# Expert slabs as two adjacent rows per partition, and a token gather in two parts with an unscaled choice matrix

## The reference, cut to what matters

```python
def expert_choice_moe(h, w_router, w_gate, w_up, w_down):
    cap = CAPACITY_FACTOR * S // N_EXPERTS            # 64 tokens for each of 16 experts
    aff = jax.nn.softmax(jnp.einsum('bsd,de->bse', h, w_router), axis=-1)
    g, idx = lax.top_k(aff.transpose(0, 2, 1), cap)   # each expert picks its tokens
    xin = jax.vmap(lambda hb, ib: hb[ib])(h, idx)     # gather
    a = jnp.einsum('becd,edf->becf', xin, w_gate)
    u = jnp.einsum('becd,edf->becf', xin, w_up)
    y = jnp.einsum('becf,efd->becd', jax.nn.silu(a) * u, w_down)
    y = y * g[..., None]
    ...
```

## Time and profile before

| | us |
|---|---|
| median of 3 runs | 2101.24 |
| the runs | 2095.47, 2101.57, 2101.24 |
| the profiled execution | 2095.03 |
| its span, first to last instruction | 2093.2 |
| TensorE matmuls busy | 2023.0 (97%) |
| VectorE, ScalarE busy | 913.4 (44%), 699.0 (33%) |
| expert stage, first matmul to the last scatter | 284.3 to 752.3 |

### The profile page before, as it was taken

The page is one execution under the profiler, slowest core; times in us unless marked ns, Lnnn a source line. Parts: engine busy times, 40 slices in busy tenths (PEclk is TensorE's granted clock), DMA queues, the critical chain, the costliest instruction groups (busy, mean ns, idle before and its releaser), DMA issues.

```text
span 2093.2 us, 23666 instructions
## 1 busy us (share of the span) xinstructions
PE 2023.0 (97%) x9843; PEld 1319.7 (63%) x9843; DVE 913.4 (44%) x1358; ACT 699.0 (33%) x1165; POOL 14.0 (1%) x28
## 2 busy tenths in 40 slices
PE   5999999999999999999999999999999899999999
PEld 4745543333333358476478887887877558888787
DVE  4474132112222144455076666336545447666433
ACT  4353211111110141275253333234442444333323
POOL 1000000000000000000000000000000000000000
PEclk9999999999999999999999999999999999999999
DMA  9459359999999962200223332232222014233211
GB/s 318 141 215 309 115 206 409 409 409 409 409 409 409 409 229 70 81 1 1 80 74 88 101 101 81 101 96 65 81 61 61 1 41 121 82 100 101 81 60 41
DMA packets 199597, 344.15 MB, mean 164 GB/s; under 512 B 15067, under 2 KB 137547, under 8 KB 196291
## 3 DMA queue, kind: packets, MB, share of 16 engines
q1 hardware_dynamic: 197872, 340.46, 45.6%
q0 software_dynamic: 944, 1.91, 0.4%
q10 hardware_dynamic: 675, 0.27, 0.1%
HBM read 340.50 MB, written 2.11 MB: 164 GB/s over the span
## 4 chain that ended last, share of the span: by engine, by line
PE 92%; DVE 3%; DMA 2%; ACT 1%; issue 1%; SPq 0%; DVEq 0%; ACTq 0%
PE bank L1871 21%; PE bank L1179 14%; PE bank L1888 12%; PE bank L1724 11%; PE bank L1740 5%; PE bank L1685 3%; PE bank L1643 3%; PE bank L727 3%; PE bank L1131 2%; PE bank L771 2%; PE bank L748 2%; DMA ring<-in_w_in 2%; PE bank L1119 1%; PE bank L1193 1%; PE bank L1752 1%; DMA hT<-in_w_down 1%
## 5 line engine op out<-in xcount | busy, mean ns | idle before, releaser
L1871 PE MATMUL bank<-h_high,ring_low 128*128 128x512 f32 x640 | 254.3, 397 | 0.0
L479 ACT ACTIVATE w_high<-ring 128x2048 fp32r<-128x2048 f32 (+1 forms) x87 | 165.2, 1903 | 227.5 <-PE bank L1871 180.9
L1871 PE MATMUL bank<-h_high,w_high 128*128 128x512 f32 x608 | 239.3, 394 | 0.0
L486 DVE TENSOR_TENSOR ring_low<-ring,w_high 128x2048 fp32r<-128x2048 f32 (+1 forms) x87 | 198.4, 2282 | 92.7 <-ACT w_high L479 92.7
L1871 PE MATMUL bank<-low_ff,w_high 128*128 128x512 f32 x608 | 238.1, 392 | 0.0
L1888 PE MATMUL bank<-ff_split,w_high 128*128 128x512 f32 x704 | 223.1, 397 | 1.6 <-DVE work L2484 1.6
L1888 PEld LDWEIGHTS bank<-ff_split,w_high 128*128 128x128 f32 x704 | 132.6, 188 | 36.3 <-DVE work L2484 2.4
L1888 PE MATMUL bank<-ff_split,ring_low 128*128 128x512 f32 x352 | 139.5, 396 | 0.0
L1871 PEld LDWEIGHTS bank<-h_high,ring_low 128*128 128x128 f32 x640 | 119.9, 187 | 27.6
L1871 PEld LDWEIGHTS bank<-h_high,w_high 128*128 128x128 f32 x608 | 114.0, 188 | 28.6
L1871 PEld LDWEIGHTS bank<-low_ff,w_high 128*128 128x128 f32 x608 | 114.0, 188 | 27.0
(11 more groups left out here) (371 smaller groups left out, 3381.0 us busy)
## 6 DMA issues: line engine op xcount, KB each, us to landing
ring<-in_ffn_w_up SPq DMA_DIRECT2D x88, 512.0 KB, 5.1
ring<-in_w_up SPq DMA_DIRECT2D x24, 1024.0 KB, 18.4
ring<-in_w_gate SPq DMA_DIRECT2D x24, 1024.0 KB, 18.5
ring<-in_w_down SPq DMA_DIRECT2D x24, 1024.0 KB, 18.5
ring<-in_ffn_w_down SPq DMA_DIRECT2D x22, 1024.0 KB, 4.7
ring<-in_w_ada SPq DMA_DIRECT2D x18, 1024.0 KB, 7.5
work<-in_w_up SPq DMA_DIRECT2D x16, 1024.0 KB, 18.4
work<-in_w_gate SPq DMA_DIRECT2D x16, 1024.0 KB, 18.1
```

The source lines that it names most:

```text
L479: act.activation(high_of(n, words), slab_view(g)[:, 0:words], ACT.Copy).then_inc(sem("split_high"), 1)
L486: dve.tensor_tensor(ring_low[:, slot_of(g), 0:words], slab_view(g)[:, 0:words], high_of(n, words).bitcast(F32), ALU.subtract).then_inc(sem ...
L1871: mm = pe.matmul(bank[n % 6][:, :], st[k], mv[k], start=(k == 0), stop=(k == len(st) - 1))
```

## The change

It does five things.

1. `moe_source` takes rows 2p and 2p + 1 of a slab to partition p: one piece of 8 KB. The transposes that feed those matmuls take every second column of a block of 256 (`turn_x_pe`, `turn_act_pe`), and gain and shift, which go by column, are brought into the same order once by 8 small matmuls and a copy (`pairs_turned`, `pair_gain`, `pair_shift`).
2. `h_tok` gets type fp32r (high part), and VectorE writes `h_tok_low`, the rest, by one subtraction for each block (`low_h`). It lies in the room of two slots of the expert slabs: 14 slots are left instead of 16.
3. `gather_pe` multiplies `hot`, unscaled and of type fp32r, by both parts: 8 matmuls for each half of the width instead of 4 float32 ones. `hot_r` and `hot_g` are gone.
4. `slots_pe` multiplies `hot` by `aff_inv` (16 affinities and the inverse norm of each token, 17 columns) in 4 float32 matmuls. It takes the place of the 16 of `slot_gain_pe` and stands ahead of the gather.
5. `slots_dve` copies gains and the inverse norm to `g_col` and `inv_slot` (5 small copies), and ScalarE's copy to `x_rows` multiplies by `inv_slot`.

```diff
-            return x[0][2 * pair + e, k0 * 2 * P:(k0 + 1) * 2 * P, :].rearrange("(k p) n -> p k n", p=P)
+            return x[0][2 * pair + e, k0 * 2 * P:(k0 + 1) * 2 * P, :].rearrange("(p k) n -> p k n", p=P)
...
-        moe_slots += [*HIGH_SLOTS, CONST_SLOT, *TAIL_SLOTS, *ring_freed, *H_SLOTS, NORM_SLOT]
+        moe_slots += [*HIGH_SLOTS, CONST_SLOT, *TAIL_SLOTS[2:], *ring_freed, *H_SLOTS, NORM_SLOT]
...
                 if k >= 2:
-                    pe.wait_ge(sem("htok_copied"), k - 1)
+                    pe.wait_ge(sem("htok_low"), k - 1)
...
             turn_x(DT - 1)
+            for n, x in enumerate((gain2, mod[:, 24:24 + DT])):
+                for j in range(2):
+                    for h in range(2):
+                        mm = pe.matmul(bank[0][HD * h:HD * h + HD, DT * n + j:DT * n + DT:2], ident[:, j::2], x[:, h:DT:2], start=True,
+                                       stop=True)
+            mm.then_inc(route_step("pairs_turned")[0], 1)
...
+            def slots_pe(i):
+
+                pe.wait_ge(sem("hot_ready"), i + 1)
+                if i:
+                    pe.wait_ge(sem("actT_copied"), 2 * i - 1)
+                for tt in range(TT):
+                    mm = pe.matmul(bank[5][:, 0:N_EXP + 1], hot[:, tt, :].bitcast(F32), aff_inv[:, tt, :], start=(tt == 0),
+                                   stop=(tt == TT - 1))
+                mm.then_inc(sem("slots_summed"), 1)
...
                 if j == 0 and half == 0:
-                    pe.wait_ge(sem("hotr_ready"), i + 1)
+                    slots_pe(i)
                 for tt in range(2 * half, 2 * half + 2):
-                    mm = pe.matmul(bank[GATHER_BANK[j]][:, :], hot_r[:, tt, :], h_tok[:, tt, S * j:S * j + S], start=(tt == 0),
-                                   stop=(tt == TT - 1))
+                    for x in (h_tok, h_tok_low):
+                        mm = pe.matmul(bank[GATHER_BANK[j]][:, :], hot[:, tt, :], x[:, tt, S * j:S * j + S],
+                                       start=(tt == 0 and x is h_tok), stop=(tt == TT - 1 and x is h_tok_low))
...
                 for k in range(4):
-                    mm = pe.transpose(bank[X_BANK[j]][:, P * k:P * k + P], x_rows[:, S * j + P * k:S * j + P * k + P], ident)
+                    c0 = S * j + HALF * (k // 2) + k % 2
+                    mm = pe.transpose(bank[X_BANK[j]][:, P * k:P * k + P], x_rows[:, c0:c0 + HALF - 1:2], ident)
...
             copy_h(DT - 1)
+            act.wait_ge(*route_step("pairs_turned"))
+            act.activation(small[:, 80:80 + 2 * DT], bank[0][:, 0:2 * DT], ACT.Copy).then_inc(route_step("pairs_copied")[0], 1)
+            act.wait_ge(*route_step("pairs_copied"))
             act.wait_ge(*route_step("logit_ready"))
...
                 act.wait_ge(sem("gathered"), 2 * i + j + 1)
-                act.activation(x_rows[:, S * j:S * j + S], bank[GATHER_BANK[j]][:, :], ACT.Copy).then_inc(sem("xrow_copied"), 1)
+                act.wait_ge(sem("slots_copied"), i + 1)
+                act.activation(x_rows[:, S * j:S * j + S], bank[GATHER_BANK[j]][:, :], ACT.Copy, scale=inv_slot[:, i % 2:i % 2 + 1])\
+                   .then_inc(sem("xrow_copied"), 1)
...
+            def low_h(k):
+                dve.wait_ge(sem("htok_copied"), k + 1)
+                at = slice(P * k, P * k + P)
+                dve.tensor_tensor(h_tok_low[:, :, at], bank[4 + k % 2][:, :].rearrange("p (i d) -> p i d", i=TT),
+                                  h_tok[:, :, at].bitcast(F32), ALU.subtract).then_inc(sem("htok_low"), 1)
...
-                dve.tensor_tensor(hot_r, hot, inverse_col.unsqueeze(2).to_broadcast([P, TT, P]), ALU.mult).then_inc(sem("hotr_ready"), 1)
-                dve.tensor_tensor(g4, h4, af2, ALU.mult).then_inc(sem("hotg_ready"), 1)
...
+            def slots_dve(i):
+                dve.wait_ge(sem("slots_summed"), i + 1)
+                for e in range(2):
+                    for c in range(2):
+                        dve.tensor_copy(g_col[HD * c:HD * c + HD, i % 2, e:e + 1],
+                                        bank[5][HD * e:HD * e + HD, 2 * i + e:2 * i + e + 1])
+                dve.tensor_copy(inv_slot[:, i % 2:i % 2 + 1], bank[5][:, N_EXP:N_EXP + 1]).then_inc(sem("slots_copied"), 1)
```

More of the change, by code:

```diff
@@ L185, in build @@
         gain1, gain2 = sb("gain1", [P, DT]), sb("gain2", [P, DT])
-        small = sb("small", [P, 96])
+        small = sb("small", [P, 104])
         SQ = 3
@@ L199, in build @@
         low_ev, low_od, low_ff = (alias(f"low_{n}", [P, DT, S], at) for n, at in (("ev", LOW_EV), ("od", LOW_OD), ("ff", LOW_FF)))
-        MOE_AT = 7168 + 2 * DT * N_EXP + 3 * TT * N_EXP + N_EXP + TT + 8 + 3 * TT * P
+        HOT_AT = 7168 + 2 * DT * N_EXP + 3 * TT * N_EXP + TT + N_EXP + TT + 8
+        MOE_AT = HOT_AT + 3 * TT * P
+        hot = alias("hot", [P, TT, P], HOT_AT)
+        h_tok = alias("h_tok", [P, TT, D])
+        h_tok_low = alias("h_tok_low", [P, TT, D], WORK - 4 * SLAB)
         pick = alias("pick", [P, S], MOE_AT)
@@ L254, in build @@
         idle_col = small[:, 78:79]
+        pair_gain, pair_shift = small[:, 80:80 + DT], small[:, 80 + DT:80 + 2 * DT]
         a = Area()
@@ L285, in build @@
         a = Area()
-        h_tok = a.take(TT, D)
+        a.take(TT, D)
         b = Area(a.at)
@@ L296, in build @@
         logit = a.take(TT, N_EXP)
-        aff = a.take(TT, N_EXP)
+        aff_inv = a.take(TT, N_EXP + 1)
+        aff = aff_inv[:, :, 0:N_EXP]
         shift_row = a.take(N_EXP)
@@ L301, in build @@
         best = a.take(8)
-        hot, hot_r, hot_g = a.take(TT, P), a.take(TT, P), a.take(TT, P)
+        assert a.at == HOT_AT
+        a.take(3, TT, P)
         assert b.at <= a.at == MOE_AT, (a.at, MOE_AT)
         x_rows = rstd[:, :, :].rearrange("p a b -> p (a b)")
-        g_col = small[:, 76:78]
+        g_col = small[:, 96:100].rearrange("p (u e) -> p u e", u=2)
+        inv_slot = small[:, 100:102]
         MOE_TAIL = WORK - 4 * SLAB
@@ L1430, in _ @@
             for g in range(MOE_0, MOE_0 + MOE_N):
[L1431 removed]
+                if g - MOE_0 < len(moe_slots) and slot_of(g) in HIGH_SLOTS:
                     sp.wait_ge(sem("in1_done"), len(in1_tiles))
[L1434 removed]
+                if g - MOE_0 < len(moe_slots) and slot_of(g) == TAIL_SLOTS[2]:
                     sp.wait_ge(*WIN_A.out(len(win_units) - 1))
@@ L1701, in turn_pick_pe @@
                 for tt in range(TT):
-                    mm = pe.transpose(bank[6][:, P * tt:P * tt + P], hot[:, tt, :], ident)
+                    mm = pe.transpose(bank[6][:, P * tt:P * tt + P], hot[:, tt, :].bitcast(F32), ident)
                 mm.then_inc(sem("pick_turned"), 1)
[L1705 to L1713, removed]
             def gate_up_pe(i, e, w):
@@ L2320, in _ @@
                                          ALU.add).then_inc(sem("out1_copied"), 1)
+                if k >= 2:
+                    low_h(k - 2)
                 if k == 0:
@@ L2325, in _ @@
                        .then_inc(route_step("gained_router")[0], 1)
+            low_h(DT - 2)
             wide_inverse(dve, "ffn")
@@ L2340, in _ @@
             dve.tensor_tensor(aff, aff, row_t.unsqueeze(2).to_broadcast([P, TT, N_EXP]), ALU.mult).then_inc(route_step("aff_ready")[0], 1)
+            dve.tensor_copy(aff_inv[:, :, N_EXP:N_EXP + 1], inverse_col.unsqueeze(2))
+            low_h(DT - 1)
             dve.wait_ge(*route_step("affT_copied"))
@@ L2407, in _ @@
                     hot_dve(i + 1)
+                    slots_dve(i + 1)
                 gated_dve(i, 1)
```

34 lines of the change are left out of this document (15 added, 19 removed).

## The result

| | before | changed |
|---|---|---|
| median of the runs, us | 2098.91 (2095.47 to 2101.57, 4 runs) | 2079.27 (2076.25 to 2082.73, 4 runs) |
| ratio, 95% interval | 1 | 0.9909 [0.9893, 0.9925] |
| span of the profiled execution, us | 2093.2 | 2078.6 |
| first gate/up matmul to first matmul of the next block, us | 468.02 | 458.09 |
| a feed-forward up stage of 960 matmuls, us (there are two) | 223.30 | 219.86 |

The kernel is 19.6 us faster, where 10.7 were forecast. The forecast, 2090.5 with a range from 2080, started from 2101.24, the median of the three runs before that were known then; a fourth run brings it to 2098.91. These 0.7 us are less than the runs scatter; what has to be explained is that the gain is nearly twice the forecast.

The account below looks back on a forecast made before the run. Slab transfers were taken to set the expert stage's end. Transfers -9.0 (-13.9 for 8 KB pieces, +5.0 for two slots fewer) and start -1.75 gave -10.7: 2090.5 us from 2101.24, range 2080 to 2104.6.

Parts of the forecast that it names:

- The transfers: Expert stage: 8 KB pieces cut a slab from 2.564 to 2.485 us, -13.9; with two more slabs to move, -9.0.
- The rate of the `w_ada` slabs with a full queue: 422 GB/s from 22 to 30 us in 8 KB pieces, taken as the changed expert stage's rate: 2.485 us a slab.
- that with the queue not full: Later `w_ada` slabs at 378 GB/s, basis of the rival that 8 KB pieces go slower: +40.8, 2142 us, chance 0.10.
- Two slots fewer, +5.0: Expert stage: with 14 slots 178 slabs must move instead of 176, two more at 2.485 us each.
- The start, -1.75: Routing and first gather ahead of the expert stage: +0.4, +0.9 and -3.05 sum to -1.75, bounds -2.2 and -0.5.
- the 3.9 of the forecast: First gather: 16 fp32r matmuls take 3.9 us instead of 6.95, -3.05.
- the late copy, +0.4: Start: the sorted gain and shift's copy precedes the affinities' exponential in ScalarE's queue, +0.4, bounds 0 and 1.2.
- The filler that hid hot_r: Start: two keep_busy matmuls hold TensorE until 275.9, so dropping hot_r (0.69 us) is worth nothing.
- the 8.3 us from the last landing: End of the expert stage: time from the last slab's landing to the next block, kept unchanged at 8.3 us.
- The work within a pair is cut, and this is worth nothing while transfers bound: Expert stage: pairs fall from 58.6 to 55.1 us on TensorE, transfers take 59.6; some 24 us saved become DMA waits.
- the range's lower end: 428 GB/s in the expert stage gives 2083.9, less 4 for the lower cluster of runs: 2080.

Follow-up runs that it names:

- e3: Changed kernel with expert pieces of 4 KB, plain-block transposes and unsorted gain and shift; 14 slots and new gather kept: 2090.31 us, ratio 0.9955.
- f2: Changed kernel with 12 slots for expert slabs instead of 14: 2084.16 us, ratio 0.9928.
- e7: Kernel before with 8 KB pieces, `small` of 104 floats and 14 slots instead of 16, old float32 gather kept: 2086.85 us, ratio 0.9935.
- g3: Changed kernel with one filler matmul instead of two ahead of the first gather: 2077.58 us, ratio 0.9898.
- f4: Kernel before with `small` of 104 floats and eight more unused floats ahead of `work`: 2095.66 us, one execution.
- e1: Kernel before with only `small` widened from 96 to 104 floats: 2091.17 us, ratio 0.9966.
- e5: Kernel before with 8 KB pieces and `small` of 104 floats, 16 slots and old float32 gather kept: 2084.96 us, ratio 0.9931.

## Why the prediction was right in the stage and wrong in the sum

**The transfers: right.** 178 slabs at 2.485 us and 6.5 us make 448.8 us from the first free slot to the last slab's matmuls; measured were 448.58. The rate of the `w_ada` slabs with a full queue was the right row to take, and that with the queue not full the wrong one. By the cost per packet in the Trainium skill, DMA: Bandwidth & Descriptors, "Why small descriptors are slow", the 8 KB pieces were 1.1% better, an estimate; e3 against the changed kernel is 2.9% (2.556 and 2.484). The limit of some 358 GB/s that the Trainium skill gives in the same page's "Where 436 GB/s comes from" (there a stack's 716 GB/s over two cores) did not bind this kernel, which runs on one core: 409 and 421 GB/s over whole pairs.

**Two slots fewer, +5.0: right** for the changed kernel (f2: +5.01 for the next two). With the old gather they would have cost nothing (e7), since the bound is then another.

**The start, -1.75: measured -2.2.** The gather took 3.79 us for the 3.9 of the forecast, the slot sums 0.96 for 0.9; the late copy, +0.4, came to 0.1 (by the timelines the ranks are turned 91.94 us after the output projection starts in the kernel before, and 92.03 in the changed one). The filler that hid hot_r before now covers the wait for hot: with one matmul less 0.54 us come back (g3).

**The end: 0.7 shorter, but not by the change.** From the start of the last slab's matmuls to the next block it was 8.19 us (744.13 to 752.32) and is 7.53 (735.38 to 742.91). The forecast kept the 8.3 us from the last landing, with the 2.99 and 2.58 us of the last groups, as if they always came with the wait of 1.98 us. They do not: in f4 the same group follows a wait of 2.06 us, in e1 one of 1.83, and takes 1.94 us in both. The waits of some 0.6 us ahead of each slab in the changed kernel did not bring the clock down either.

In all: -2.20 for the start, -9.27 from the first slab issued to the last one's matmuls (457.85 to 448.58), -0.66 for the end, which is the -12.1 measured. Without the end it is -11.5, to be held against the -10.7 of the forecast.

**"The work within a pair is cut, and this is worth nothing while transfers bound": wrong as a step, though the stage's sum holds.** The condition was taken for given. The earlier trace rows already had the number against it: TensorE was busy for 453.1 of 457.8 us, so faster transfers alone had 4.6 us to gain. e5 and e7 show it: 462.6 instead of 458.1 us. The old gather would have cost the changed kernel 4.5 us in the stage; with pieces of 4 KB the new one gives hardly anything (e3: 470.90, where the 467.42 of e1 and two slabs of 2.56 more make 472.5). Nor does what TensorE saves turn into waits: of the 17.6 us that it works less (453.13 to 435.56), waits take up 8.4, and the other 9.2 are what this stretch is shorter by. Neither part is worth its own price alone, and the two are not to be added.

**The step that failed and put the result outside the range: the wider `small`, costed at nothing.** The change makes `small` eight floats longer and so moves all that lies behind it; the sum (-9.0 for the transfers, -1.75 for the start) has no term for it, and no bound. It is worth 7.8 us by the two chain rows, 8.5 by e1's median. No row of the kernel before shows that a place has a price, so the amount could not be read ahead. What could be read is how much lay open: the range's lower end came from one DMA rate and 4 us of scatter, and left nothing for the 690 us of feed-forward stages, of which 1% is 7 us.

## What to carry to other kernels

Before calling one resource the bound, write the second one's busy time beside it: the difference is all that relief of the first can give, and a cut in the second that looks idle is what lets the rest through. Where hundreds of microseconds of matmuls run back to back, a change in any tile's size moves the tiles behind it and here shifted their pace by up to 3%; when a stage that nobody touched changes its length, compare its count and length in the chain of waits first, and test by padding alone. Here sixteen more floats of padding were worth 11.4 us in the feed-forward, more than the 10.7 that the whole change was forecast to bring.

## What the runs showed of the hardware that was not expected

- The pace of back-to-back fp32r matmuls goes by the place of their operands in SBUF: 960 in 217.62 to 223.90 us, 522 in 118.63 to 122.56, each value coming back to 0.03 us wherever a place is repeated, at a granted clock of 1.00. The Trainium skill, SBUF — State Buffer, "Who interferes with whom", says that TensorE never waits on anyone; the trace agrees in that it shows no idle time on it in the up stage, and yet its pace moves by 2.9%.
- A queue kept full by the same slabs in pieces of 8 KB instead of 4 gives 421 instead of 409 GB/s, and a slab takes a median of 26.5 us to land (`w_down` in `ring`, 29 slabs) instead of 18.5 (24 slabs): by an estimate from these times and 2.48 and 2.56 us a slab, some 11 in flight instead of 7.
- Where the granted clock falls varies from one execution of the same kernel to the next (the two rows at 90 to 112 us: 24 matmuls in 7.40 or 5.83 us), and what is lost there carries into the rest of the span. A wait of 1.98 us was followed by a clock of 0.64 in one execution, and waits of 1.83 and 2.06 us at the same place by the full clock in two others (e1, f4).
